# A two-block transformer: the sums of c times w_ada as chained multiply-adds on VectorE, and on ScalarE with GpSimd for eight of 28 units

## The chip, the core and the metric

The kernel runs on one core of a Trainium2 chip. A core has five engines that each work through an instruction list of their own and wait for each other by semaphores: TensorE (PE, matrix products), VectorE (DVE), ScalarE (ACT), GpSimd (POOL) and SyncE (SP), which here only issues DMAs. The metric is the time of one execution on the device, in microseconds (us).

## The reference

```python
# first block, D = 1024, 256 tokens
mod = silu(c) @ w_ada + b_ada          # (1024) x (1024 x 9216): nine vectors of 1024
sh1, sc1, gt1, sh2, sc2, gt2, sh3, sc3, gt3 = split(mod, 9)
n = rmsnorm(h, g_ffn1) * (1 + sc1) + sh1
h = h + 0.5 * gt1 * ((silu(n @ w1_gate) * (n @ w1_up)) @ w1_down)   # inner width 2816
n = rmsnorm(h, g_mix) * (1 + sc2) + sh2
h = h + gt2 * hybrid_mixer(n, w_in, w_pool, pool_scale, w_out)      # "pool" mixer below
n = rmsnorm(h, g_ffn2) * (1 + sc3) + sh3
h = h + 0.5 * gt3 * ((silu(n @ w2_gate) * (n @ w2_up)) @ w2_down)
h = rmsnorm(h, g_final)
# second block: two attention layers, with mixers called "window" and "causal", and a last norm
```

Half of the first mixer pools over windows of 2 to 16 tokens, the other half is attention with 8 heads. All is float32.

## The kernel before

All weights come through the core in units of 1 MB (128 partitions x 2048 floats): 256 columns of a weight matrix, or 256 rows of a down matrix. Unit u is loaded by SP into `raw[u % 3]` (`load_unit`), rounded to float32r by ScalarE (`whi`, `high(u)`, line 554), and VectorE makes the rest that the rounding lost (`wlo = raw - whi`, `low(u)`, line 814). TensorE then makes three products for each (`nhi,whi`, `nlo,whi`, `nhi,wlo`; lines 1133 to 1135), 48 instructions for a unit. Unit u + 3 can be loaded when `low(u)` is done, for it takes the same slot.

The stages are: eight units of w_ada at the start, a norm, the first feed-forward network (units 0 to 32: gate, up and down of eleven blocks; the blocks after the first are a loop of ten rounds, j = 0 to 9, on each engine), a norm, the pool mixer (units 33 to 44), a norm, the second feed-forward network, a norm, and the window and causal mixers.

The vector `mod` is made beside this work, in 36 units a of w_ada (each 1024 x 256, also 1 MB). Units 0 to 7 come at the start. Units 8 to 18 are needed by the end of the first feed-forward network, 19 to 31 up to the end of the pool mixer, 32 to 35 by the end of the second network. One unit takes four steps:

1. `load_ada(a)` on SP loads it into one of two slots of `ada`, and first waits until the slot's last user is summed (`macc_done`).
2. The product with silu(c), in place: on GpSimd in one instruction (line 467, `prod_done`), or, for 21, 22, 23, 25, 27, 29 and 31, on ScalarE in eight, one for each of the eight chunks of 128 rows (line 591, `aprod_done`).
3. `reduce_products(a)` on VectorE adds the eight chunks in one instruction over 128 x 2048 (line 866, into `macc`).
4. `mod_sum(a)` on TensorE sums over the partitions by two one-column products with ones (line 1163), and `mod_out` on VectorE adds b_ada.

The order within a mixer is written out by hand, once for all engines, in the list `order` of `mixer_plan`: U, K, V, Q and W are projections (each takes a unit, but W), SC the scores and the softmax of four heads, TPV transposes and the products with V, OUTA, OUTB and OUT the output projection, MACa the steps 2 and 3 of the units a and a + 1, MODa step 4 of both. Each engine does its part of each entry in this order and skips what isn't its own. After a projection ScalarE copies the result out of PSUM and then makes `high(u + 3)`, and VectorE makes `low(u + 3)`. SP's loads are in one queue, in the order of the units, with the loads of w_ada placed between them by the table `ada_after` (unit of the mixer: the units of w_ada that are loaded behind it).

Of the kernel before, what the change touches and what calls it, by code (L numbers as in the profile page):

```python
# [1537 lines left out]
```

## Time and profile before

| | |
|---|---|
| time, median of 3 runs | 897.82 us (896.24 to 899.46) |
| profiled execution: span of its instructions | 896.2 us |
| time of the profiled execution | 896.24 us, by the run that equals the span |
| TensorE busy | 767.6 us, 86% |
| VectorE busy | 620.1 us, 69% |
| ScalarE busy | 404.1 us, 45% |
| GpSimd busy | 162.6 us, 18% |
| chain that ended last, by engine | PE 68%, DVE 15%, ACT 7%, issue 6% |
| VectorE's subtractions, line 814 | 104 x 2569 ns |
| VectorE's reductions, line 866 | 32 x 3804 ns |
| moved | 152.56 MB |

A matmul's record is longer than its pitch, since matmuls overlap: within a unit one follows another every 0.12 us at the full clock. So a busy TensorE means only that it never waited. "Idle before" in a timeline names who ended the wait. Times within the span are counted from its start.

### The profile page before, as it was taken

Reading aid. Unit: us, or ns where it says so; the run is one execution under the profiler, and the core shown is the slowest. Engines: PE = TensorE matmul, PEld = TensorE weight load, DVE = VectorE, ACT = ScalarE, POOL = GpSimd, SP = SyncE. Lnnn points to the kernel's source line nnn. Section 1 sums busy time; section 2 is a strip of 40 time slices with the busy share of each in tenths; the row PEclk is TensorE's granted clock in tenths of the full one; section 3 lists DMA queues with packets and bytes.
Section 4 is the critical chain, followed back from the end, with each engine's and each line's share of the span. In section 5 each row is a group of like instructions: output and inputs, shape, how many; then the busy total and the mean of one; then the engine's idle time right before and its main releaser. Section 6 shows DMA issues by size and latency. Waiting matters only on the chain.

```text
span 896.2 us, 14391 instructions
## 1 busy us (share of the span) xinstructions
PE 767.6 (86%) x5800; PEld 720.6 (80%) x5800; DVE 620.1 (69%) x775; ACT 404.1 (45%) x645; POOL 162.6 (18%) x87
## 2 busy tenths in 40 slices
PE   4279999999959868738999999996799988999995
PEld 3279999999949866637999999994777777888884
DVE  5987877887878877677549447446567756577641
ACT  5353433343426735434444333335365553554542
POOL 3621114223245551234004000001000000000000
PEclk9579999999978978878999999998899999999998
DMA  9877777678653944065557655552133224422201
GB/s 299 269 261 240 252 248 234 222 237 270 221 173 98 325 141 142 31 222 194 189 187 234 208 189 170 184 187 93 53 119 113 94 95 141 141 95 95 95 1 47
DMA packets 132451, 152.56 MB, mean 170 GB/s; under 512 B 2616, under 2 KB 126268, under 8 KB 132284
## 3 DMA queue, kind: packets, MB, share of 16 engines
q1 hardware_dynamic: 132324, 152.01, 52.0%
q8 instruction: 26, 0.43, 0.2%
q14 instruction: 13, 0.11, 0.0%
q10 hardware_dynamic: 88, 0.02, 0.0%
HBM read 150.97 MB, written 1.05 MB: 170 GB/s over the span
## 4 chain that ended last, share of the span: by engine, by line
PE 68%; DVE 15%; ACT 7%; issue 6%; DMA 2%; POOL 1%; SPq 0%; DVEq 0%; ACTq 0%; POOLq 0%
PE sc L1133 10%; PE sc L1135 9%; PE sc L1134 9%; PE acc L1133 9%; PE acc L1134 8%; PE acc L1135 8%; DVE macc L866 6%; ACT whi L554 2%; DVE wlo L814 2%; PE stat L1144 1%; DMA ada<-in_w_ada_dram 1%; PE acc L1281 1%; DVE rstd L834 1%; PE acc L1244 1%; ACT prob L656 1%
## 5 line engine op out<-in xcount | busy, mean ns | idle before, releaser
L814 DVE TENSOR_TENSOR wlo<-raw,whi 128x2048 fp32r<-128x2048 f32 x104 | 266.9, 2569 | 110.8 <-ACT whi L554 110.8
L554 ACT ACTIVATE whi<-raw 128x2048 fp32r<-128x2048 f32 x105 | 199.9, 1905 | 80.8 <-PE sc L1135 76.5
L1133 PE MATMUL sc<-nhi,whi 128*128 128x256 f32 x704 | 202.7, 288 | 9.5 <-DVE nlo L853 6.3
L1134 PE MATMUL sc<-nlo,whi 128*128 128x256 f32 x704 | 201.2, 286 | 0.0
L1135 PE MATMUL sc<-nhi,wlo 128*128 128x256 f32 x704 | 201.2, 286 | 0.0
L1133 PEld LDWEIGHTS sc<-nhi,whi 128*128 128x128 f32 x704 | 137.4, 195 | 10.2 <-issue 6.7
L467 POOL TENSOR_TENSOR ada<-ada,cT 128x2048 f32<-128x2048 f32 x21 | 92.5, 4408 | 256.4 <-DMA ada<-in_w_ada_dram 256.4
L1134 PEld LDWEIGHTS sc<-nlo,whi 128*128 128x128 f32 x704 | 137.3, 195 | 0.0
L1135 PEld LDWEIGHTS sc<-nhi,wlo 128*128 128x128 f32 x704 | 137.1, 195 | 0.0
L1133 PE MATMUL acc<-nhi,whi 128*128 128x256 f32 x376 | 117.0, 311 | 16.6 <-DVE nlo L853 12.2
L866 DVE TENSOR_REDUCE macc<-ada 128x256 f32<-128x2048 f32 x32 | 120.8, 3804 | 5.7 <-POOL ada L467 3.4
L1134 PE MATMUL acc<-nlo,whi 128*128 128x256 f32 x376 | 110.1, 293 | 0.0
L1135 PE MATMUL acc<-nhi,wlo 128*128 128x256 f32 x376 | 109.8, 292 | 0.0
L1133 PE MATMUL acc<-hhi,whi 128*128 128x256 f32 x352 | 101.0, 287 | 4.1 <-DVE hlo L1028 4.1
L1134 PE MATMUL acc<-hlo,whi 128*128 128x256 f32 x352 | 100.2, 285 | 0.0
L1135 PE MATMUL acc<-hhi,wlo 128*128 128x256 f32 x352 | 100.0, 284 | 0.0
L1133 PEld LDWEIGHTS acc<-nhi,whi 128*128 128x128 f32 x376 | 75.8, 202 | 25.6 <-issue 18.2
L1134 PEld LDWEIGHTS acc<-nlo,whi 128*128 128x128 f32 x376 | 76.2, 203 | 1.9 <-issue 1.9
L1135 PEld LDWEIGHTS acc<-nhi,wlo 128*128 128x128 f32 x376 | 75.9, 202 | 0.0
L1133 PEld LDWEIGHTS acc<-hhi,whi 128*128 128x128 f32 x352 | 67.3, 191 | 4.5 <-DVE wlo L814 2.6
L1134 PEld LDWEIGHTS acc<-hlo,whi 128*128 128x128 f32 x352 | 67.5, 192 | 0.1
L1135 PEld LDWEIGHTS acc<-hhi,wlo 128*128 128x128 f32 x352 | 67.4, 191 | 0.0
(164 smaller groups left out, 1189.8 us busy)
## 6 DMA issues: line engine op xcount, KB each, us to landing
ada<-in_w_ada_dram SPq DMA_DIRECT2D x32, 1024.0 KB, 5.1
raw<-in_w_gate_dram SPq DMA_DIRECT2D x22, 1024.0 KB, 5.7
raw<-in_w_up_dram SPq DMA_DIRECT2D x22, 1024.0 KB, 5.4
raw<-in_w_down_dram SPq DMA_DIRECT2D x22, 1024.0 KB, 4.9
raw<-in_w_out_dram SPq DMA_DIRECT2D x12, 1024.0 KB, 5.0
raw<-in_w_in_b_dram SPq DMA_DIRECT2D x10, 1024.0 KB, 5.1
raw<-in_w_in_a_dram SPq DMA_DIRECT2D x9, 1024.0 KB, 5.3
raw<-in_w_in_dram SPq DMA_DIRECT2D x8, 1024.0 KB, 7.8
```

The lines of the kernel that those rows point to most:

```text
L467: nc.gpsimd.tensor_tensor(to, to, c_mul, ALU.mult).then_inc(prod_done, 1)
L554: nc.scalar.activation(whi[:, u % NS], raw[:, u % NS], ACT.Copy).then_inc(hi_done, 1)
L656: ins = nc.scalar.activation(prob[:, s, lo:up], prob[:, s, lo:up], ACT.Exp, bias=nm[:, s, b:b + 1], accum_out=den[:, s, b:b + 1])
L814: nc.vector.tensor_tensor(wlo[:, u % NS], raw[:, u % NS], whi[:, u % NS].bitcast(F32), ALU.subtract).then_inc(lo_done, 1)
L834: link(nc.vector.reciprocal(rstd[:, :], std[:, :]))
L866: nc.vector.tensor_reduce(macc[:, slot], src.rearrange("p c n -> p n c"), AX_X, ALU.add).then_inc(macc_done, 1)
L1133: mm(to, stat_hi, mov_hi, start=first, stop=False, skip_group_check=True)
L1134: mm(to, stat_hi, mov_lo, start=False, stop=False, skip_group_check=True)
L1135: return mm(to, stat_lo, mov_hi, start=False, stop=last, skip_group_check=True)
L1144: mm(ss_ps, ones[:, :], src, start=first, stop=last).then_inc(ss_done, 1)
L1244: mm(rot_ps[:, :], rotation, src[:, :, :].rearrange("p b n -> p (b n)"), start=True, stop=True).then_inc(rot_done, 1)
L1281: mm(to[part, 0:S], vv[:, 0, col:col + HD], probT[:, h % 2, 0:S], start=True, stop=False, skip_group_check=True)
```

## The change

Three things are changed.

Most units of w_ada from 8 on (`BY_DVE`: 8 to 19, 24, 26, 28, 30 and 32 to 35) are now made on VectorE alone by `multiply_add`: one multiplication by c of the first chunk, and seven `scalar_tensor_tensor` (chunk times c plus the sum so far), each of 128 x 256 and each waiting for the one before (`part_done`). No product on GpSimd or ScalarE is made for them. The other eight (`BY_POOL`: 20 to 23, 25, 27, 29, 31) have their product on ScalarE, as eight instructions, and the sum on GpSimd, as three additions of 1024, 512 and 256 elements in a partition (`add_parts`), with semaphores of their own. Units 20 to 23 move from the mixer into the first feed-forward loop: ScalarE makes their products behind its rounds 0, 3, 5 and 7, and SP's loop is cut behind its rounds 2, 4 and 6 for the loads of 21, 22 and 23. The mixer's list and the table of loads are new.

```diff
-            order = ["U0", "MAC20", "U1", "K0", "MOD20", "MAC22", "K1", "V0", "MOD22", "MAC24", "Q0", "V1",
-                     "SC0", "W0", "W1", "MOD24", "MAC26", "Q1", "TPV0", "SC1", "OUTA", "MOD26", "TPV1", "MAC28",
-                     "OUTB", "OUT1", "MOD28", "MAC30", "OUT2", "MOD30", "OUT3"]
+            order = ["U0", "MAC24", "U1", "K0", "MOD24", "K1", "MAC26", "V0", "Q0", "MOD26", "V1", "SC0", "W0", "W1",
+                     "MAC28", "Q1", "TPV0", "SC1", "OUTA", "MOD28", "TPV1", "MAC30", "OUTB", "OUT1", "MOD30", "OUT2",
+                     "OUT3"]
-ADA_SLOT = {a: 1 if 9 <= a < 20 else a % 2 for a in range(MOD_START, MOD_UNITS)}
+BY_POOL = (20, 21, 22, 23, 25, 27, 29, 31)
+BY_DVE = tuple(a for a in range(MOD_START, MOD_UNITS) if a not in BY_POOL)
+ADA_SLOT = {a: 0 if a in BY_POOL or a in (8, 32, 34) else 1 for a in range(MOD_START, MOD_UNITS)}
...
# SP, load_ada: the wait for the slot's last user
+                if n in BY_POOL:
+                    sp.wait_ge(pmacc_done, BY_POOL.index(n) + 1)
+                elif n is not None:
+                    sp.wait_ge(macc_done, MOD_START + BY_DVE.index(n) + 1 + (reps if reps is not None else 0))
# SP, first feed-forward network
+                    load_ada(20)
                     sp.dma_start(consts[:, P:C_END], shape_consts[:, P:C_END]).then_inc(tables_in, 16)
-                for start, end in ((1, FB - 1),) if first else ((0, 4), (4, FB - 1)):
+                for start, end in ((1, 3), (3, 5), (5, 7), (7, FB - 1)) if first else ((0, 4), (4, FB - 1)):
...
+                    if first and end < FB - 1:
+                        load_ada(21 + (end - 3) // 2)
...
-                    ada_after = {3 * FB: (19,), 3 * FB + 1: (20,), 3 * FB + 2: (21,), 3 * FB + 5: (22, 23), 3 * FB + 7: (24, 25),
-                                 3 * FB + 9: (26, 27), 3 * FB + 10: (28, 29), 3 * FB + 11: (30, 31)}
+                    ada_after = {3 * FB: (19,), 3 * FB + 1: (24,), 3 * FB + 2: (25,), 3 * FB + 4: (26, 27),
+                                 3 * FB + 6: (28, 29), 3 * FB + 9: (30, 31)}
# GpSimd
-            product(8)
-            product(9)
-            with pool.Fori(0, FB - 1) as j:
-                product(10, reps=j)
+            for a in (20, 21, 22, 23):
+                add_parts(a)
...
+            def add_parts(a):
+                part, n = ada[:, ADA_SLOT[a]], BY_POOL.index(a)
+                pool.wait_ge(aprod_done, MOD_START // 2 + n + 1)
+                link(nc.gpsimd.tensor_tensor(part[:, 0:4], part[:, 0:4], part[:, 4:8], ALU.add))
+                link(nc.gpsimd.tensor_tensor(part[:, 0:2], part[:, 0:2], part[:, 2:4], ALU.add))
+                if n >= 2:
+                    pool.wait_ge(pmod_cols, n - 1)
+                nc.gpsimd.tensor_tensor(macc[:, 2 + n % 2], part[:, 0], part[:, 1], ALU.add).then_inc(pmacc_done, 1)
# ScalarE, first feed-forward loop
+                for start, end in ((0, 1), (1, 4), (4, 6), (6, 8), (8, FB - 1)) if f == 0 else ((0, FB - 1),):
...
+                    if end < FB - 1:
+                        product({1: 20, 4: 21, 6: 22, 8: 23}[end])
# VectorE
+            def multiply_add(a, reps=None):
+                n, add = BY_DVE.index(a), reps if reps is not None else 0
+                part, to = ada[:, ADA_SLOT[a]], macc[:, macc_slot(a)]
+                dve.wait_ge(ada_in[ADA_SLOT[a]], ada_landings(a) + 16 * add)
+                dve.wait_ge(mod_cols, MOD_START + n - 1 + (1 if reps is not None else 0) + add)
+                for ch in range(DC):
+                    if ch == 0:
+                        ins = nc.vector.tensor_scalar(to, part[:, ch], cT[:, ch:ch + 1], None, ALU.mult)
+                    else:
+                        dve.wait_ge(part_done, 7 * n + ch + 7 * add)
+                        ins = nc.vector.scalar_tensor_tensor(out=to, in0=part[:, ch], scalar=cT[:, ch:ch + 1], in1=to,
+                                                             op0=ALU.mult, op1=ALU.add)
+                    if ch < DC - 1:
+                        ins.then_inc(part_done, 1)
+                ins.then_inc(macc_done, 1)
# TensorE, first feed-forward loop, cut behind rounds 2, 5, 7 and 9
+                    if f == 0:
+                        n = {3: 0, 6: 1, 8: 2, FB - 1: 3}[end]
+                        mod_sum(20 + n, mod3_ps[:, 2 * n:2 * n + 2])
```

Besides, `fgain` (the last norm's gain) now lies in a slot of `ada` and is loaded ahead of the causal mixer, and `mod_out(20, 4)` writes the four moved units behind the first network.

SP's queue in the first feed-forward loop. Before, from the loop's start to its end (lines 370 are weight units, 378 a unit of w_ada):

```order
L370 ISA [waits lo_done]
L370 DMA raw<-in_w_gate_dram 128x8x256
L369 REGISTER_ALU
L370 DMA raw<-in_w_up_dram 128x8x256 [waits lo_done]
L369 REGISTER_ALU
L370 ISA [waits lo_done]
L370 DMA raw<-in_w_down_dram 128x2x1024
L377 REGISTER_ALU
L378 ISA [waits macc_done]
L378 DMA ada<-in_w_ada_dram 128x8x256
L414 REGISTER_ALU
L414 COMPARE_AND_BRANCH
```

Now, from the middle of round 4 (the second of the four loops) to the start of round 5 (386 are weight units, 397 units of w_ada):

```order
L386 DMA raw<-in_w_down_dram 128x2x1024
L396 REGISTER_ALU
L397 ISA [waits macc_done]
L397 DMA ada<-in_w_ada_dram 128x8x256
L434 REGISTER_ALU
L434 COMPARE_AND_BRANCH
L397 DMA ada<-in_w_ada_dram 128x8x256 [waits pmacc_done]
L434 UNCONDITIONAL_BRANCH
L434 ISA
L386 ISA [waits lo_done]
L386 DMA raw<-in_w_gate_dram 128x8x256
```

A load that waits for GpSimd's sum of the unit before (`pmacc_done`) now stands between the weight units of round 4 and those of round 5. The same stands behind rounds 2 and 6.

SP's queue in the pool mixer, from the load of unit 35 (K0) on. Before:

```order
L370 DMA raw<-in_w_in_dram 128x8x256 [waits lo_done]
L378 DMA ada<-in_w_ada_dram 128x8x256 [waits macc_done]
L370 DMA raw<-in_w_in_dram 128x8x256 [waits lo_done] x3
L378 DMA ada<-in_w_ada_dram 128x8x256 [waits macc_done] x2
L370 DMA raw<-in_w_in_dram 128x8x256 [waits lo_done] x2
L378 DMA ada<-in_w_ada_dram 128x8x256 [waits macc_done] x2
L370 DMA raw<-in_w_out_dram 128x8x256 [waits lo_done] x2
L378 DMA ada<-in_w_ada_dram 128x8x256 [waits macc_done] x2
```

Now:

```order
L386 DMA raw<-in_w_in_dram 128x8x256 [waits lo_done]
L397 DMA ada<-in_w_ada_dram 128x8x256 [waits pmacc_done]
L386 DMA raw<-in_w_in_dram 128x8x256 [waits lo_done] x2
L397 DMA ada<-in_w_ada_dram 128x8x256 [waits macc_done]
L397 DMA ada<-in_w_ada_dram 128x8x256 [waits pmacc_done]
L386 DMA raw<-in_w_in_dram 128x8x256 [waits lo_done] x2
L397 DMA ada<-in_w_ada_dram 128x8x256 [waits macc_done]
L397 DMA ada<-in_w_ada_dram 128x8x256 [waits pmacc_done]
L386 DMA raw<-in_w_in_dram 128x8x256 [waits lo_done]
```

Unit 38 (Q0) stood ahead of the first pair of w_ada and now stands behind one (26, 27); unit 40 (Q1) stood ahead of the second pair and now stands behind it (28, 29).

VectorE in the same place, from `low(36)` behind U0 to the softmax. Before:

```order
L814 TENSOR_TENSOR wlo<-raw,whi 128x2048 [waits hi_done,tables_in]
L866 TENSOR_REDUCE macc<-ada 128x256 [waits mod_cols,prod_done]
L866 TENSOR_REDUCE macc<-ada 128x256 [waits mod_cols,aprod_done]
L814 TENSOR_TENSOR wlo<-raw,whi 128x2048 [waits hi_done] x2
L875 TENSOR_TENSOR mod<-sc,biasT 128x4 [waits mod_cols]
L866 TENSOR_REDUCE macc<-ada 128x256 [waits mod_cols,aprod_done] x2
L814 TENSOR_TENSOR wlo<-raw,whi 128x2048 [waits hi_done] x2
```

Now:

```order
L838 TENSOR_TENSOR wlo<-raw,whi 128x2048 [waits hi_done,tables_in]
L897 TENSOR_SCALAR macc<-ada,cT 128x256 [waits mod_cols,ada_in1]
L900 SCALAR_TENSOR_TENSOR macc<-ada,cT,macc 128x256 [waits part_done] x7
L838 TENSOR_TENSOR wlo<-raw,whi 128x2048 [waits hi_done] x2
L923 TENSOR_TENSOR mod<-sc,biasT 128x4 [waits mod_cols,pmod_cols]
L838 TENSOR_TENSOR wlo<-raw,whi 128x2048 [waits hi_done]
L897 TENSOR_SCALAR macc<-ada,cT 128x256 [waits mod_cols,ada_in1]
L900 SCALAR_TENSOR_TENSOR macc<-ada,cT,macc 128x256 [waits part_done] x7
L838 TENSOR_TENSOR wlo<-raw,whi 128x2048 [waits hi_done] x2
L923 TENSOR_TENSOR mod<-sc,biasT 128x4 [waits mod_cols,pmod_cols]
```

Two reductions have become a chain of eight instructions, and `low(39)` now stands ahead of the second of them.

## Rows read from the trace of the kernel before

**Rows 1.** Busy time by stretch; columns: stretch, length, PE, PEld, DVE, ACT, POOL, PEclk, DMA share, GB/s.

```profile
59.00:268.00 209.00, 197.92 (x1598) 196.25 (x1598) 167.53 (x92) 76.31 (x65) 56.69 (x19) 0.97 0.72 238
268.00:418.00 150.00, 109.33 (x731) 99.58 (x731) 115.24 (x133) 75.53 (x148) 61.90 (x43) 0.83 0.53 172
```

**Rows 2.** Waits of PE from 262 to 420; columns: us in total, times, longest.

```profile
PE sc L1163 <- DVE macc L866: 15.5, 5, 11.5
PE sc L1163 <- DVE mx L926: 11.7, 2, 6.8
```

**Rows 3.** Timeline, first network, rounds 3 and 4; columns: start, us, instruction, idle before.

```profile
129.36 0.37 SPq L378 DMA_DIRECT2D ada<-in_w_ada_dram  x1
131.60 0.37 SPq L370 DMA_DIRECT2D raw<-in_w_gate_dram  x1
...
138.69 1.90 ACT L554 ACTIVATE whi<-raw 128x2048 fp32r<-128x2048 f32 x1
144.85 1.90 ACT L554 ACTIVATE whi<-raw 128x2048 fp32r<-128x2048 f32 x1
...
142.90 3.87 DVE L866 TENSOR_REDUCE macc<-ada 128x256 f32<-128x2048 f32 x1
146.79 2.29 DVE L814 TENSOR_TENSOR wlo<-raw,whi 128x2048 fp32r<-128x2048 f32 x1
...
155.53 0.50 PE L1163 MATMUL stat<-ones,macc 128*128 128x1 f32 x4
155.90 0.36 PE L1133 MATMUL sc<-nhi,whi 128*128 128x256 f32 x1
```

**Rows 4.** ScalarE's eight products of one unit, and the landing of w_ada's loads.

```profile
279.47 3.30 ACT L591 ACTIVATE ada<-ada,cT 128x256 f32<-128x256 f32 x8
...
DMA to landing us min/median/max: 4.9/5.1/10.1
```

**Rows 5.** Busy time by stretch, behind TensorE's waits (ended 246.9 and 311.9).

```profile
247.00:250.00 3.00, 3.00 (x15) 3.00 (x16) 3.00 (x1) 1.05 (x2) 3.00 (x1) 0.50 0.59 185
307.00:313.00 6.00, 3.19 (x26) 2.87 (x24) 2.58 (x2) 5.12 (x10) 3.45 (x1) 0.88 1.09 347
313.00:316.00 3.00, 3.00 (x15) 2.50 (x12) 3.00 (x2) 0.47 (x1) 0.00 (x0) 0.50 0.19 45
316.00:322.00 6.00, 6.00 (x45) 5.87 (x45) 5.79 (x12) 0.33 (x1) 1.26 (x2) 0.81 0.96 322
```

**Rows 6.** Timeline, GpSimd against VectorE, by a norm behind the second network.

```profile
621.26 0.85 POOL L476 TENSOR_TENSOR std<-sq 128x256 f32<-128x256 f32 x1 [7.36 <-ACT sq L565]
...
621.45 0.95 DVE L842 SCALAR_TENSOR_TENSOR hT<-hT,gainT,rstd 128x256 f32<-128x256 f32 x1
...
L842 DVE SCALAR_TENSOR_TENSOR hT<-hT,gainT,rstd x8: 473/480/947, 619.9 to 624.0; 128x256 f32<-128x256 f32 x8
```

**Rows 7.** Timeline, ends of the start and of the first network.

```profile
53.16 3.60 POOL L467 TENSOR_TENSOR ada<-ada,cT 128x2048 f32<-128x2048 f32 x1 [6.98 <-DMA ada<-in_w_ada_dram]
54.64 6.47 DVE L814 TENSOR_TENSOR wlo<-raw,whi 128x2048 fp32r<-128x2048 f32 x2 [1.39 <-ACT whi L554]
58.96 0.58 PE L1133 MATMUL sc<-nhi,whi 128*128 128x256 f32 x1 [3.19 <-DVE wlo L814]
...
246.63 5.69 DVE L814 TENSOR_TENSOR wlo<-raw,whi 128x2048 fp32r<-128x2048 f32 x1
```

**Rows 8.** Timeline, pool mixer.

```profile
281.88 7.68 DVE L866 TENSOR_REDUCE macc<-ada 128x256 f32<-128x2048 f32 x2
283.34 0.61 POOL L510 TENSOR_TENSOR pw<-pw 128x256 f32<-128x256 f32 x1
...
358.70 4.47 DVE L946 TENSOR_SCALAR prob<-prob,rden 128x128 f32<-128x128 f32 x2
399.50 0.99 PE L1163 MATMUL sc<-ones,macc 128*128 128x1 f32 x4 [11.54 <-DVE macc L866]
411.62 0.88 DVE L828 SCALAR_TENSOR_TENSOR hT<-acc,mod,hT 128x256 f32<-128x256 f32 x2 [1.31 <-PE acc L1135]
```

More of the change, by code:

```diff
@@ L157, in by_act, with macc_slot @@
 def by_act(a):
-    return (a < MOD_START or 20 <= a < 32) and a % 2 == 1 or a == 22
+    return a % 2 == 1
 def products(a, act):
     return sum(by_act(n) == act for n in range(a + 1))
+def macc_slot(a):
+    if a < MOD_START:
+        return a % 2
+    if a in BY_POOL:
+        return 2 + BY_POOL.index(a) % 2
+    return 1 if 9 <= a < 20 else BY_DVE.index(a) % 2
 def slot_before(a):
-    return max([n for n in range(MOD_START, a) if ADA_SLOT[n] == ADA_SLOT[a]], default=-1) + 1
+    return max([n for n in range(MOD_START, a) if ADA_SLOT[n] == ADA_SLOT[a]], default=None)
 FFN_UNIT = (0, 3 * FB + 12)
@@ L192, in build @@
         ada = sb("ada", [P, 2, DC, UC])
-        macc = sb("macc", [P, 2, UC])
+        macc = sb("macc", [P, 4, UC])
         hT = sb("hT", [P, DC, S])
@@ L519, in pooling @@
                 pool.wait_ge(pooled, g + 1)
-            product(20)
             add_squares(1)
@@ L536, in _ @@
                         bias(h)
-                elif st["kind"] == "MAC" and st["i"] > 20 and not by_act(st["i"]):
-                    product(st["i"])
+                elif st["kind"] == "MAC":
+                    add_parts(st["i"] + 1)
             add_squares(2)
-            for a in range(32, MOD_UNITS):
-                product(a)
             for k in range(3, 6):
@@ L706, in mixer @@
                     elif st["kind"] == "MAC":
-                        if by_act(st["i"]):
-                            product(st["i"])
                         product(st["i"] + 1)
@@ L855, in normalise, with reduce_products @@
                                                        op1=ALU.subtract).then_inc(nlo_done, 1)
-            def reduce_products(a, reps=None):
-                add = reps if reps is not None else 0
-                dve.wait_ge(aprod_done if by_act(a) else prod_done, products(a, by_act(a)) + add)
-                slot = a % 2 if a < MOD_START else ADA_SLOT[a]
-                last = max([n for n in range(a) if (n % 2 if n < MOD_START else ADA_SLOT[n]) == slot], default=-1)
-                if last >= 0:
-                    dve.wait_ge(mod_cols, last + 1 + add)
-                src = start_slots[a % 5] if a < MOD_START else ada[:, slot]
-                nc.vector.tensor_reduce(macc[:, slot], src.rearrange("p c n -> p n c"), AX_X,
-                                        ALU.add).then_inc(macc_done, 1)
+            def reduce_products(a):
+                dve.wait_ge(aprod_done if by_act(a) else prod_done, products(a, by_act(a)))
+                if a >= 2:
+                    dve.wait_ge(mod_cols, a - 1)
+                nc.vector.tensor_reduce(macc[:, a % 2], start_slots[a % 5].rearrange("p c n -> p n c"), AX_X,
+                                        ALU.add).then_inc(macc_done, 1)
@@ L869, in mod_out @@
             def mod_out(a, count=2, reps=None):
                 n = 2 * count
-                dve.wait_ge(mod_cols, a + count + (reps if reps is not None else 0))
-                ps = mod0_ps if a == 0 else (mod2_ps if 19 <= a < 32 and reps is None or a == 34 else mod1_ps)[:, 0:n]
+                if a == 20 or a in (24, 26, 28, 30):
+                    dve.wait_ge(pmod_cols, BY_POOL.index(a + count - 1) + 1)
+                if a >= MOD_START and a != 20:
+                    dve.wait_ge(mod_cols, MOD_START + BY_DVE.index(a if a < 32 else a + 1) + 1 +
+                                (reps if reps is not None else 0))
+                elif a == 0:
+                    dve.wait_ge(mod_cols, MOD_START)
@@ L874, in mod_out @@
+                if a == 0:
+                    ps = mod0_ps
+                elif a == 20:
+                    ps = mod3_ps
+                else:
+                    ps = (mod2_ps if 19 <= a < 32 and reps is None or a == 34 else mod1_ps)[:, 0:n]
                 at = 2 * a if reps is None else reps * 2 + 2 * a
@@ L1068, in ffn @@
                     mod_out(19, 1)
-                    dve.wait_ge(mod_done, 20)
+                    mod_out(20, 4)
+                    dve.wait_ge(mod_done, 24)
                     link(coefficient(1))
@@ L1158, in mod_sum @@
             def mod_sum(a, to, reps=None):
-                pe.wait_ge(macc_done, a + 1 + (reps if reps is not None else 0))
-                slot = a % 2 if a < MOD_START else ADA_SLOT[a]
+                if a in BY_POOL:
+                    pe.wait_ge(pmacc_done, BY_POOL.index(a) + 1)
+                else:
+                    n = a if a < MOD_START else MOD_START + BY_DVE.index(a)
+                    pe.wait_ge(macc_done, n + 1 + (reps if reps is not None else 0))
+                slot = macc_slot(a)
                 for n in range(2):
@@ L1440, in ffn @@
                     mod_sum(8, mod1_ps[:, 0:2])
-                for start, end in ((0, FB - 1),) if f == 0 else ((0, 3), (3, FB - 1)):
+                for start, end in ((0, 3), (3, 6), (6, 8), (8, FB - 1)) if f == 0 else ((0, 3), (3, FB - 1)):
                     with pe.Fori(start, end) as j:
```

66 lines of the change are left out of this document (34 added, 32 removed).

## The prediction, written before the changed kernel ran

> **What bounds the kernel now.** I read the stretches first, then TensorE's waits, then the timelines of the engines on which those waits end, and last the two instruction queues that the diff cuts. In the first network TensorE is busy for 197.9 of 209 us at a granted clock of 0.97 [rows 1]: it sets the pace, and whatever VectorE, ScalarE or GpSimd save inside its loop is worth nothing, while whatever makes a weight unit late there costs in full. The pool mixer is the opposite: TensorE works 109.3 of 150 us, VectorE 115.2 [rows 1], and TensorE's two largest waits are for `macc`, 15.5 us, and for the softmax's maxima, 11.7 us [rows 2]. There a change in the sums of w_ada can gain.
>
> **The chain of eight against the reduction.** An in-place reduction has a pitch of 7.68 / 2 = 3.84 us [rows 8]. A `scalar_tensor_tensor` of 128 x 256 takes 0.48 us [rows 6], and the next must wait for it; with some 0.04 us between two that is 0.52, times seven 3.64, and the first multiplication at most 0.48: about 4.1 us. So on VectorE one unit costs what it cost before, +0.3 us, and the gain lies in the count: the mixer now has four units on VectorE instead of twelve (24, 26, 28, 30), and no product in front of them. Bounds: 3.2 us if the eight overlapped like independent ones, 5 us if the wait costs twice 0.04 and the loop's register instructions are not hidden.
>
> But these instructions read two SBUF operands. With a GpSimd addition beside it, such an instruction took 0.95 instead of 0.48 us [rows 6]: 0.47 us more for an addition of 256 elements (0.61 us in this form [rows 8]). The reductions at 281.88 took 3.84 us each while GpSimd worked in short steps beside them [rows 8], the same as elsewhere. Now GpSimd's sum is three additions: 0.61 us for 256 elements [rows 8] and 3.60 for 2048 [rows 7] give 1.67 ns an element, so 1.9, 1.0 and 0.6 us, 3.8 with gaps. Where both run they take turns, one chained step for one GpSimd instruction. The Trainium skill ("SBUF — State Buffer", Who interferes with whom) says this as a rule: a DVE instruction with two SBUF inputs and a GpSimd instruction that reads SBUF block each other fully, a reduction never contends. By that rule the change trades a form that never waits for one that does; the row at 621.45 agrees.
>
> **First network, start: -2.1 us.** The product of unit 8 (3.60 us from 53.16) held up `low(1)`, two of which took 6.47 us instead of 4.4, and TensorE waited for it until 58.96 [rows 7]. Without that product TensorE starts 2.0 to 2.1 us earlier. SP's queue now waits for unit 8's sum before `load_ada(20)`; the units behind it land some 2 us later, which the 7 us between a unit's rounding and its use cover.
>
> **Its loop, TensorE's own part: +1.1 us.** `mod_sum` takes 0.37 us (155.53 to 155.90 [rows 3]); three of the four new ones stand inside, the fourth falls into the wait behind the loop.
>
> **Its loop, SP's queue: +15.0 us.** This term decides. SP runs ahead of ScalarE: behind its round 4 (w_ada at 129.36) it issues unit 17 at 131.60 [rows 3], as soon as `low(14)` has freed the slot. In the changed kernel `load_ada(22)` stands between, and waits for GpSimd's sum of unit 21. Its product is behind ScalarE's round 3, whose last `high(16)` runs from 138.69 to 140.6 [rows 3]; eight products take 3.30 us [rows 4], so 143.9; the sum takes 3.8 us, with VectorE's own chain beside it (the reduction stood at 142.90 [rows 3]) 4.8: 148.7. Unit 22 lands 5.1 us later [rows 4], unit 17 behind it: 1.05 MB at 347 GB/s [rows 5] is 3.0 us, so 156.9. Then 1.9 us for `high` and 2.3 for `low` with their gaps: 161.1. TensorE wants it at 155.90 [rows 3]: it waits 5.2 us. Today `high(17)` runs at 144.85. After such a wait the clock is at half: granted 0.50 for at least 3.0 us behind a wait of 2.5, and 0.50 then 0.81 over 9 us behind one of 3.0 [rows 5], which costs 1.6 to 3.2 us; I take 2.3. Behind round 6 it is the same again (`load_ada(23)` waits for unit 22's sum, behind ScalarE's round 5). Behind round 2 it is not: unit 20's product follows round 0, and its sum is done before SP arrives. So 2 x (5.2 + 2.3) = 15.0. Bounds: with no turns taken and a late loss of 1.6, 2 x (4.2 + 1.6) = 11.6; with 3.3 us for a megabyte and 3.2 for the clock, 2 x (6 + 3.2) = 18.4.
>
> **End of the loop: -2.6 us.** The last `low` took 5.69 us beside a GpSimd product [rows 7], 3.4 more than alone; without it the chain for unit 19 (+0.3) ends earlier, and with it the residual, by about 3.5 us of which 0.9 are already in the two small terms above.
>
> **Pool mixer: +9.0 us.** All times here are counted as in the trace of before, as if the mixer began where it does there. `low(36)` ends at 281.9, where the reductions began [rows 8]. The chain for unit 24 now meets GpSimd's pooling (0.61 us a step) and its sum of unit 25: eight steps, eight turns, end at 291.2 instead of 286.0; sum 25 at 291.7. Only then does SP load 26, 27, and behind them units 38 and 39, which land at 302.2 and 305.1. VectorE stands in `low(38)`, then `low(39)` (309.3), then the chain for 26 beside sum 27: 316.4. Behind that SP loads 28, 29, 40, 41; unit 41 lands at 330.3, `low(41)` ends at 334.5, and only after it `mod_out(26)`, for which the scores wait: 334.7, against 311.9 before [rows 5]: +22.8. Then it gains: GpSimd's product no longer holds the softmax (-2.7). Unit 43 is the third such victim (behind 30 and 31, which wait for 28 and 29): ScalarE has `high(43)` before the second softmax, now +26.8. That softmax gains 3.0: its scaling took 4.47 us beside a product [rows 8]. +23.7 when unit 30's chain begins; it ends at 404.1. TensorE's waits of 11.5 us [rows 8] and 2.4 are gone, and three output steps of residual, `high` and `low`, 5.5 us each, lead to the last residual at 420.6, against 411.62 [rows 8]: +9.0. The same walk with no turns taken gives scores at +15.8 and the last residual at 408.4: -3.2. With 3.3 us a megabyte it is +12.
>
> **The rest: 0.** In the second network the same number of units is on VectorE, TensorE never waits there today, and units 32 to 35 have no GpSimd work beside them. The two attention layers keep their instructions; the gain's load is 0.5 MB where DMA is mostly idle.
>
> Sum: -2.1 + 1.1 + 15.0 - 2.6 + 9.0 = +20.4 on the span of 896.2 of an execution that itself took 896.2, so 916.6; the median of the runs is 1.6 us above that one: 918.
>
> **Rivals.** *The loads come late, but taking turns costs nothing.* For it: the row at 621.45 is one pair of small instructions. Against it: it fits. 11.6 - 3.2 - 3.6 = +4.8: 903. *The loop is covered, the mixer is not.* This needs unit 17 to have 5 us more slack than rows 3 give; against it the order of the queue, which is fixed. -3.6 + 9.0 = +5.4: 903. *Faster: TensorE is not held in the loop and the mixer keeps its gain.* One mechanism, the slack of the weight units: if loads issued 17 us late still arrive before TensorE needs them (a pair of units deep in `raw` and `whi`), only the savings are left: -3.6 - 3.2 = -6.8, so 891. It decides when unit 17 lands before 151.7; that needs sum 21 at 143.6, before its product is even done at 143.9. For it speaks only that the mixer's waits for `macc` (15.5 us) and GpSimd's 92 us of products vanish. *The chain costs 5 us instead of 4.1*: in the loop VectorE has over 3 us of idle time a round, in the mixer +1 for each of four: 921.
>
> **Chances.** Forecast (both late loads and turns taken) 0.60, either of the two alone 0.22, faster 0.15, otherwise slower 0.03. Three runs of this kernel tell about 0.3% (2.7 us). The range must reach over the two at 903 and leaves out the faster one: 902 to 926. Faster by over 0.3%: 0.15; within: 0.03; slower: 0.82.
>
> **What the profile would show.** In the first network: SP's units 17 and 23 issued about 17 us after the rhythm, TensorE waiting some 5 us for `wlo` before two of ten rounds, and a lower clock behind both. GpSimd's additions and VectorE's chained steps stretched to 0.9 us and more wherever they meet. In the mixer: `high(38)`, `high(40)` and `high(43)` ended by a DMA, scores of the first softmax some 20 us late against the mixer's start, no wait of 11 us before the last output step. I am wrong if TensorE runs through the loop, or if the chained steps stay at 0.5 us beside GpSimd.

## The result, and the profile after

The changed kernel takes 914.4 us (median of 4 runs, 913.6 to 915.8) against 898.6 us (896.2 to 899.6) for the kernel before in the same session: ratio 1.0186, 95% interval 1.0168 to 1.0205. It is slower by 15.8 us; the forecast was 918 us, range 902 to 926.

In the changed kernel's profile the lines have new numbers: L838 is `low`, L577 `high`, L897 and L900 VectorE's chain, L491, L492 and L495 GpSimd's three additions, L614 ScalarE's products, L386 and L397 the loads of weight units and of w_ada, L1216 `mod_sum`, L923 `mod_out`, L852 the residual, L1313 the scores. Among the costliest groups (busy time, mean ns of one | idle before) the chain shows its price at once: 140 steps, 666 ns each on the mean, though a step alone takes some 480.

```profile
L900 DVE SCALAR_TENSOR_TENSOR macc<-ada,cT,macc 128x256 f32<-128x256 f32 x140 | 93.2, 666 | 5.0
```

Busy time by stretch (columns of [rows 1]): the first stretch of [rows 1], the mixer from norm to norm, and the stretches behind TensorE's two long waits of the loop:

```profile
59.00:268.00 209.00, 193.57 (x1588) 192.86 (x1587) 146.68 (x167) 87.10 (x89) 19.37 (x12) 0.97 0.70 233
275.93:431.94 156.01, 105.33 (x714) 95.77 (x714) 85.59 (x148) 65.20 (x123) 51.46 (x49) 0.81 0.46 147
...
159.60:163.00 3.40, 3.40 (x20) 3.40 (x19) 3.05 (x3) 2.76 (x3) 0.00 (x0) 0.58 1.10 351
202.70:206.00 3.30, 3.23 (x15) 3.24 (x16) 3.20 (x3) 3.11 (x3) 0.00 (x0) 0.50 1.06 343
```

GpSimd and VectorE have much less to do than before (GpSimd 19.4 instead of 56.7 us in the first stretch, VectorE 85.6 us in the mixer, where it had 115.2 from 268 to 418 [rows 1]), yet TensorE is busy for less of the first stretch: the time went into waits. Behind the two long ones its clock was granted at 0.58 and 0.50, so for most of these stretches at the lower of its two levels: matmuls start every 0.21 us instead of 0.12, which costs 1.5 us behind the first wait (until 162.4) and 1.9 us behind the second (until 206.8). TensorE's waits from 60 to 270, then from 262 to 460 (us in total, times, longest), where [rows 2] had `macc` and `mx`:

```profile
PE sc L1182 <- DVE wlo L838: 11.8, 2, 6.3
...
PE sc L1313 <- DVE mod L923: 17.6, 1, 17.6
PE sc L1313 <- DVE mx L974: 9.3, 1, 9.3
PE acc L1182 <- ACT kraw L648: 6.7, 1, 6.7
```

The first wait of the loop, followed backwards through the timeline of the changed kernel, at the place of [rows 3]:

```profile
126.50 20.30 SPq L397 DMA_DIRECT2D ada<-in_w_ada_dram  x2
147.13 0.37 SPq L386 DMA_DIRECT2D raw<-in_w_gate_dram  x1
...
138.02 3.29 ACT L614 ACTIVATE ada<-ada,cT 128x256 f32<-128x256 f32 x8
154.69 1.91 ACT L577 ACTIVATE whi<-raw 128x2048 fp32r<-128x2048 f32 x1 [12.21 <-DMA raw<-in_w_gate_dram]
...
141.39 2.69 POOL L491 TENSOR_TENSOR ada<-ada 128x1024 f32<-128x1024 f32 x1 [48.50 <-ACT ada L614]
144.16 1.35 POOL L492 TENSOR_TENSOR ada<-ada 128x512 f32<-128x512 f32 x1
145.59 0.80 POOL L495 TENSOR_TENSOR macc<-ada 128x256 f32<-128x256 f32 x1
...
122.70 3.61 DVE L900 SCALAR_TENSOR_TENSOR macc<-ada,cT,macc 128x256 f32<-128x256 f32 x7
140.81 6.91 DVE L900 SCALAR_TENSOR_TENSOR macc<-ada,cT,macc 128x256 f32<-128x256 f32 x7
141.85 2.51 DVE L900 SCALAR_TENSOR_TENSOR macc<-ada,cT,macc 128x256 f32<-128x256 f32 x1
156.63 2.29 DVE L838 TENSOR_TENSOR wlo<-raw,whi 128x2048 fp32r<-128x2048 f32 x1 [8.91 <-ACT whi L577]
...
159.06 0.58 PE L1182 MATMUL sc<-nhi,whi 128*128 128x256 f32 x1 [5.49 <-DVE wlo L838]
```

SP's two w_ada loads span 20.3 us, because the second stands until GpSimd's sum of unit 21 ends at 146.4; only then is unit 17 issued (147.13; before, 131.60 [rows 3]). ScalarE gets it 12.2 us after it ran out of work, TensorE 5.5 us after it wanted it. The chain without a GpSimd sum beside it takes 3.61 us for seven steps (122.70), beside one 6.91 (140.81). The third step of that chain, 141.85, alone took 2.51 us: it ends only when GpSimd's long addition (141.39, 2.69 us) has ended.

In the mixer the same thing stands in front of the first scores:

```profile
300.50 4.22 SPq L397 DMA_DIRECT2D ada<-in_w_ada_dram  x2
304.76 1.86 SPq L386 DMA_DIRECT2D raw<-in_w_in_dram  x2
326.88 0.99 SPq L397 DMA_DIRECT2D ada<-in_w_ada_dram  x2
327.92 1.42 SPq L386 DMA_DIRECT2D raw<-in_w_in_dram  x1
...
312.51 1.92 ACT L577 ACTIVATE whi<-raw 128x2048 fp32r<-128x2048 f32 x1 [12.04 <-DMA raw<-in_w_in_dram]
338.11 1.91 ACT L577 ACTIVATE whi<-raw 128x2048 fp32r<-128x2048 f32 x1 [17.08 <-DMA raw<-in_w_in_dram]
...
301.67 2.65 POOL L495 TENSOR_TENSOR macc<-ada 128x256 f32<-128x256 f32 x1
...
293.94 6.53 DVE L900 SCALAR_TENSOR_TENSOR macc<-ada,cT,macc 128x256 f32<-128x256 f32 x7
300.39 3.35 DVE L838 TENSOR_TENSOR wlo<-raw,whi 128x2048 fp32r<-128x2048 f32 x1
406.07 6.63 DVE L900 SCALAR_TENSOR_TENSOR macc<-ada,cT,macc 128x256 f32<-128x256 f32 x7
428.80 0.87 DVE L852 SCALAR_TENSOR_TENSOR hT<-acc,mod,hT 128x256 f32<-128x256 f32 x2
...
345.58 0.81 PE L1313 MATMUL sc<-kd,qT 64*128 64x128 f32 x4 [17.61 <-DVE mod L923]
```

Units 38 and 40 reach ScalarE 12 and 17 us after it ran out of work, each loaded (304.76 and 327.92) behind a w_ada pair that waited for a chain and a sum. GpSimd's last addition, of 256 elements (0.61 us alone [rows 8]), took 2.65 us against a `low` of 2048 elements, and that `low` 3.35 instead of 2.29.

To compare kernels I cut each profiled run where ScalarE takes the root of a norm (the `std` rows; before at 264.90, 413.83 and 617.56, changed at 275.93, 431.94 and 635.67). Each number in this table is a difference of two such rows, the last one of the span and the third row.

| kernel | first network | pool mixer | second network | rest | median, us |
|---|---|---|---|---|---|
| before | 264.9 | 148.9 | 203.7 | 278.6 | 898.6 |
| changed | 275.9 | 156.0 | 203.7 | 276.9 | 914.4 |
| e1, products early | 260.0 | 156.1 | 203.7 | 276.9 | 900.4 |
| e2, mixer's loads later | 277.1 | 132.0 | 203.9 | 276.8 | 890.7 |
| e3, both | 261.6 | 132.2 | 203.9 | 276.7 | 875.3 |
| e4, before with the chain alone | 261.9 | 149.0 | 203.8 | 276.9 | 895.2 |
| e5, e3, TensorE takes four units | 260.9 | 135.1 | 204.0 | 279.4 | 880.8 |
| e6, e3, one addition of three | 259.8 | 121.2 | 203.9 | 276.9 | 864.9 |
| e7, e3, chain before K1 | 260.5 | 131.5 | 204.0 | 279.0 | 875.5 |
| e8, e3, MOD24 later | 259.7 | 128.4 | 203.8 | 276.9 | 874.0 |
| e9, changed, one addition of three | 263.4 | 143.8 | 204.8 | 278.2 | 892.0 |
| e10, e8, reductions in the mixer | 260.1 | 129.0 | 205.2 | 277.9 | 872.5 |

The stretches behind the mixer move by up to 3 us between runs of kernels whose code there is the same, so they carry no cause, and a difference below that between two medians is not read as one either. The first network moves too: e1, e3, e5, e7, e8 and e10 have the same code there and took 259.7 to 261.6 us, a spread that arises for the most part ahead of the loop (VectorE's first chain starts at 58.91 in e1 and at 60.20 in e3). The mixer agrees within 0.2 us where its code is the same (changed and e1, e2 and e3). The change costs +11.0 us in the first network and +7.1 in the mixer.

### The profile page after: what moved, and what is told of

It reads as the page before. It is cut to its first block, busy times and chain, and to the rows that moved or that the text cites. A ratio compares the mean times of both kernels' runs of the same rounds, so it can differ in the third digit from the quotient of the medians.

```text
span 912.6 us, 14572 instructions
## 1 busy us (share of the span) xinstructions
PE 764.7 (84%) x5800; PEld 717.6 (79%) x5800; DVE 569.0 (62%) x906; ACT 407.6 (45%) x653; POOL 104.3 (11%) x90
## 4 chain that ended last, share of the span: by engine, by line
PE 43%; ACT 4%; DVE 4%; issue 1%; POOL 0%; DVEq 0%; ACTq 0%; POOLq 0%
PE acc L1182 6%; PE acc L1183 6%; PE acc L1184 6%; PE sc L1182 5%; PE sc L1184 5%; PE sc L1183 5%; PE stat L1193 1%; PE acc L1334 1%; PE acc L1297 1%; PE acc L1376 1%; PE acc L1377 1%; PE acc L1378 1%; ACT whi L577 1%; DVE rstd L858 1%; ACT prob L679 1%
## 5 line engine op out<-in xcount | busy, mean ns | idle before, releaser
L838 DVE TENSOR_TENSOR wlo<-raw,whi 128x2048 fp32r<-128x2048 f32 x104 | 239.2, 2301 | 171.9 <-ACT whi L577 171.8
L577 ACT ACTIVATE whi<-raw 128x2048 fp32r<-128x2048 f32 x105 | 200.0, 1905 | 137.0 <-PE sc L1184 62.9
L1182 PE MATMUL sc<-nhi,whi 128*128 128x256 f32 x704 | 203.7, 289 | 19.1 <-DVE wlo L838 12.8
L900 DVE SCALAR_TENSOR_TENSOR macc<-ada,cT,macc 128x256 f32<-128x256 f32 x140 | 93.2, 666 | 5.0
L504 POOL TENSOR_TENSOR std<-sq 128x256 f32<-128x256 f32 x5 | 3.8, 759 | 365.9 <-ACT sq L588 365.9
```

Of the source, the lines that this page charges most:

```text
L577: nc.scalar.activation(whi[:, u % NS], raw[:, u % NS], ACT.Copy).then_inc(hi_done, 1)
L838: nc.vector.tensor_tensor(wlo[:, u % NS], raw[:, u % NS], whi[:, u % NS].bitcast(F32), ALU.subtract).then_inc(lo_done, 1)
L900: ins = nc.vector.scalar_tensor_tensor(out=to, in0=part[:, ch], scalar=cT[:, ch:ch + 1], in1=to, op0=ALU.mult, op1=ALU.add)
L1182: mm(to, stat_hi, mov_hi, start=first, stop=False, skip_group_check=True)
```

## The experiments

**e1: only ScalarE's products move.**

```
-  for start, end in ((0, 1), (1, 4), (4, 6), (6, 8), (8, FB - 1)) if f == 0 ...
+  for start, end in ((0, 1), (1, 3), (3, 5), (5, 7), (7, FB - 1)) if f == 0 ...
-      product({1: 20, 4: 21, 6: 22, 8: 23}[end])
+      product({1: 20, 3: 21, 5: 22, 7: 23}[end])
```

> The changed kernel, only ScalarE's products of units 20 to 23 stand behind its rounds 0, 2, 4 and 6 of the first network instead of 0, 3, 5 and 7, so that the sums of 21 and 22 are done when SP's queue reaches the w_ada loads that wait for them. Theory A (two w_ada loads hold the weight units in SP's queue): both waits of TensorE for wlo in the loop (11.8 us with the one at 159.06 and the one at 202.76) go, and with them the low clock behind each (about 2 x 1.5 us); the first network ends about 14 us earlier, the mixer is as long as it was, time near 900 us. Rival B (what the loop lost is VectorE's chain taking turns with GpSimd's sums and ScalarE's 3.3 us products in the way): the same four products and sums still stand in the loop, so no more than 3 us come back, 911 us.

Measured: 900.4 us, ratio to before 1.002 (1.0002 to 1.0038). TensorE's waits from 60 to 262, all that there are:

```profile
PE sc L1216 <- DVE macc L900: 2.8, 1, 2.8
PE stat L1193 <- POOL std L504: 2.6, 1, 2.6
PE acc L1182 <- DVE hlo L1075: 0.8, 1, 0.8
```

Both waits for `wlo` are gone, though all four products and sums still stand in the loop and four of its chains still take 6.9 us. The first network ends 16.0 us earlier than in the changed kernel: 11.8 us of waits, 3.3 us of lower clock behind them (1.5 and 1.9), and 0.7 us by which this run entered the loop earlier (first chain at 58.91, changed 59.60); 0.2 us is left over. By the medians the gain is 14.1 us. Theory A holds: with the product one round earlier, the sums and their chains cost TensorE no wait in the loop, though they are as long as before.

**e2: only the mixer's w_ada loads move, and e3: both.**

```
-  3 * FB + 4: (26, 27), 3 * FB + 6: (28, 29), 3 * FB + 9: (30, 31)}
+  3 * FB + 6: (26, 27), 3 * FB + 9: (28, 29), 3 * FB + 11: (30, 31)}
```

> The changed kernel, only the mixer's w_ada pairs stand further back in SP's queue: (26, 27) behind unit 39 instead of 37, (28, 29) behind 42 instead of 39, (30, 31) behind 44 instead of 42. Theory A: TensorE's wait of 17.6 us before the first scores goes nearly whole, since units 38 to 41 no longer wait for the sums of 24 to 27; the waits behind it (6.7 and 9.3 us) shrink too; 18 us less, 896 us, with the loop's stalls as they were. Rival B (the mixer is held by the chained steps that take turns with GpSimd, not by the loads): each chain stays beside a sum of GpSimd and takes 6.5 to 7 us as now, the first scores move by under 5 us, 909 us.

> Both of the above. The places are 100 us apart, so under theory A the gains add: 14 + 18 = 32 us, 882 us, which would be 16 us faster than the kernel before. Rival: the mixer's gain is covered in part once the loop is quick (other clock); 888 us.

Measured: e2 890.7 us, ratio 0.990 (0.987 to 0.993); e3 875.3 us, ratio 0.974 (0.970 to 0.977). TensorE's waits in e2's mixer that answer to the changed kernel's 17.6 and 9.3, and the one for GpSimd's sum (3.2 there); the 6.7 us for `kraw` are as they were:

```profile
PE sc L1313 <- DVE mod L923: 3.5, 1, 3.5
...
PE sc L1216 <- POOL macc L495: 3.3, 1, 3.3
PE sc L1313 <- DVE mx L974: 2.9, 1, 2.9
```

The mixer is 24.0 us shorter than the changed kernel's, and 17 shorter than the one before, which is what the change gives when its loads do not stand in the way. I had said 18: the maxima's wait (9.3 to 2.9, unit 43 no longer late) gave more than I allowed. In e3 the two gains add up (16 + 24 = 40 in theory, 39.1 measured). Rival B failed in e2: the chains are still 6.5 and 6.9 us long there.

**e4: the kernel before, with the chain alone.** Units 8 to 19 and 32 to 35 by VectorE's chain, GpSimd's products of them gone (shortened):

```
+  CHAIN = tuple(range(8, 20)) + tuple(range(32, 36))
   def reduce_products(a, reps=None):
+      if a in CHAIN: ... tensor_scalar, then seven scalar_tensor_tensor as in multiply_add
-  product(8); product(9); with pool.Fori(0, FB - 1) as j: product(10, reps=j)    # GpSimd
```

> The kernel before, with one part of the change alone: units 8 to 19 and 32 to 35 are summed by VectorE's chain of eight instead of GpSimd's product and a reduction; the mixer, the order of the loads and the units in each loop are as before. By my terms the start gains 2.1 us and the end of the first network's loop 2.6 us, the chain's own 0.3 us a unit is hidden: 894 us. Rival (a chain of waits is dear, 5 us or more a unit, and the loop feels it): 898 us or above.

Measured: 895.2 us, ratio 0.996 (0.994 to 0.998). The chain is worth a small gain by itself; the rival is out. The first network gains 3.0 us, less than the 4.7 of my two terms. The loop's end shows a reason (VectorE, then GpSimd):

```profile
243.12 5.55 DVE L812 TENSOR_TENSOR wlo<-raw,whi 128x2048 fp32r<-128x2048 f32 x1 [1.11 <-ACT whi L552]
...
242.91 3.60 POOL L471 TENSOR_TENSOR ada<-ada,cT 128x2048 f32<-128x2048 f32 x1 [200.60 <-DMA ada<-in_w_ada_dram]
```

GpSimd's product of unit 20, the mixer's first, now starts here and takes the place of the loop's last one: `low` waits again, 5.55 us instead of 2.29. In the changed kernel unit 20 is summed inside the loop, so this cannot happen there: its last `low` (260.34) takes 2.29 us. With nothing held in the loop (e1 and the five others) the first network gains 3.3 to 5.2 us against before; my small terms said 2.1 - 1.1 + 2.6 = 3.6. The 1.7 us by which e4 falls short lie within the spread between runs, so its rows show the mechanism and not what it costs.

**e9: the changed kernel, with one GpSimd addition of three.**

```
-  link(nc.gpsimd.tensor_tensor(part[:, 0:4], part[:, 0:4], part[:, 4:8], ALU.add))
-  link(nc.gpsimd.tensor_tensor(part[:, 0:2], part[:, 0:2], part[:, 2:4], ALU.add))
```

> The changed kernel as it is, with GpSimd's first two additions of each of the eight sums left out (those sums hold two of eight parts); the order of the loads is untouched. My prediction's terms: turns cost 12.2 us of the mixer (+9.0 with them, -3.2 without) and 2 x 1.0 us of the loop's waits; here the sum of a unit is 0.8 instead of 4.8 to 6.9 us, which also brings each blocked load 3 us forward. So the loop loses 2 x 4 us less, the mixer 12 us less: 896 us. Rival (turns were over-sized by me: the mixer measured +6.2 instead of +9.0 and each pair's load waits for VectorE's chain anyway): 4 us in the loop, 5 in the mixer, 905 us.

Measured: 892.0 us, ratio to before 0.994 (0.993 to 0.996), so 22.5 us less than the changed kernel. This kernel leaves out two of three additions, so its sums hold two of eight parts. TensorE's waits, loop and mixer:

```profile
PE sc L1180 <- DVE wlo L836: 2.3, 2, 1.3
...
PE sc L1311 <- DVE mod L921: 17.7, 1, 17.7
PE sc L1311 <- DVE mx L972: 9.0, 1, 9.0
```

The mixer is 12.3 us shorter; I had put the turns at 12.2, but e9 takes away more than turns: each sum's own 4 us go as well. The loop gives back 12.5 instead of 8: 9.5 us of waits, and most of the 3.3 us of lower clock, which did not follow waits of 1.0 and 1.3 us. The long waits for `mod` and `mx` stay, since the pairs still stand in front of the units. The rival's 905 is out. What the two long additions cost (their length and the turns together) comes on top of the late loads: 12.3 us of the mixer here, 11.0 with the loads moved (e6). How much of it is turns alone, no run shows.

**e6: the same on e3.**

> Built on the kernel with both moves. Of GpSimd's three additions for each of the eight units only the last (256 elements) is done; the first two, of 1024 and 512 elements, are left out, so those sums hold two of eight parts. Theory A (one chained step waits for one GpSimd addition, the long ones above all): the four chains of the mixer fall from 6.5 to 6.9 us to about 4.2; each pair is ready 2.5 us earlier; of the four places the waits of TensorE before the first scores (3.5 us) and for the maxima (2.9 us) give some back: 871 us. Rival B (turns cost nothing, chains are long for another reason): chains stay at 6.5 us, time within 1 us of 875.

Measured: 864.9 us, ratio 0.963 (0.960 to 0.966). The mixer's four chains took 4.88, 4.33, 4.09 and 4.05 us instead of 6.53, 6.92, 6.50 and 6.63, as theory A said, but the mixer lost 11.0 us, not 4. I had looked at the chains alone. In e3 GpSimd's sum also runs beside `low` (2.65 us for its last addition), and TensorE waits 3.3 us for the sum itself at MOD24; in e6 that wait is gone, one of 3.3 us for ScalarE's `sq` at the norm behind the mixer is 1.3, and the mixer's mean granted clock is 0.89 instead of 0.85. The wait before the first scores, where I had looked for a gain, is 4.2 instead of 3.5 us.

**e5: TensorE takes units 25, 27, 29 and 31 itself.**

```
+  if a in BY_PE:
+      for n in range(2):
+          for ch in range(DC):
+              ins = mm(to[:, n:n + 1], ada[:, 0, ch, n * P:(n + 1) * P], cT[:, ch:ch + 1],
+                       start=(ch == 0), stop=(ch == DC - 1))
```

> Built on the kernel with both moves. Units 25, 27, 29 and 31 of the mixer are taken by TensorE straight from w_ada (sixteen matmuls with one column of c each, added up in PSUM) instead of ScalarE's eight products, GpSimd's three additions and two matmuls with ones. Theory A (VectorE's chain takes turns with GpSimd's sum: 6.5 to 6.9 us for seven steps beside it, 3.61 alone): with no sum beside them all four chains of the mixer show 3.6 us; ScalarE loses 13 us of products; TensorE gets 4 x 14 matmuls more, at about 0.2 us each some 11 us, mostly while it would wait anyway: 872 us against 875. Rival B (the long chains come from the DMA traffic or ScalarE's work, not from GpSimd): chains stay at 6.5 us, and TensorE's 11 us are added, 884 us.

ScalarE's products and GpSimd's sums of these four units are gone too.

Measured: 880.8 us, ratio 0.980 (0.978 to 0.983), 5.5 us slower than e3; of this the mixer shows 2.9, the rest lies behind it, where the code is the same. Two rows of VectorE from the timeline of e5's mixer, and one of its groups by line (busy time, mean ns of one | idle before):

```profile
302.87 3.62 DVE L899 SCALAR_TENSOR_TENSOR macc<-ada,cT,macc 128x256 f32<-128x256 f32 x7
339.83 3.61 DVE L899 SCALAR_TENSOR_TENSOR macc<-ada,cT,macc 128x256 f32<-128x256 f32 x7
```

```profile
L1212 PE MATMUL sc<-cT,ada 128*128 128x1 f32 x128 | 17.3, 269 | 0.0
```

The 64 matmuls are 128 records, two each. Three of the four chains fell to 3.6 us with the loads unchanged (the first, beside GpSimd's pooling, to 4.76), so the DMA traffic had not stretched them; nor had ScalarE, since in e6 its products stand and the chains fall too. But TensorE paid 17.3 us instead of my 11, in a place where it was not only waiting. Both theories failed on the sum; the mechanism of A held, its price of a matmul did not.

**e7 and e8: other places for MAC26 and MOD24.**

```
   e3:  "K0", "MOD24", "K1", "MAC26", "V0"
   e7:  "K0", "MAC26", "K1", "MOD24", "V0"
   e8:  "K0", "K1", "MOD24", "MAC26", "V0"
```

> Built on the kernel with both moves. In the mixer's order, MAC26 stands before K1 and MOD24 behind it (K0, MAC26, K1, MOD24, V0 instead of K0, MOD24, K1, MAC26, V0). TensorE waited 3.25 us at MOD24 for GpSimd's sum of unit 25 (290.20) and ran 4 us at half clock behind it, and VectorE was idle from 292.4 to 301.4 while the chain of 26 came later at 303.98. My theory (the turns reach TensorE through this wait for the sum and through the first scores' wait of 3.5 us for the sum of 27): both waits go and about 2 us of low clock with them, 9 us, 866 us. Rival (the mixer is set by ScalarE's queue and the softmax): under 2 us, 874.

> Built on the kernel with both moves. Only MOD24 moves one job back (K0, K1, MOD24, MAC26, V0), so TensorE asks for the sums of 24 and 25 one job of 6 us later. My theory: the waits of 0.68 and 3.25 us and 2 us of low clock behind them go, the chain of 26 starts 5 us earlier since K1 does: 5 us, 870 us. Rival (what is won before the first scores is lost in their wait for the sum of 27, now longer): under 2 us, 874.

Measured: e7 875.5 us, ratio 0.976 (0.972 to 0.980), which is no gain on e3; e8 874.0 us, 0.975 (0.972 to 0.979). e8's mixer is 3.7 us shorter in its profiled run, but the medians cannot tell it from e3. Its rival is borne out: the wait of `mod` before the first scores fell from 3.5 to 0.4 us, and the one for GpSimd's sums grew from 3.3 to 7.5, now for the sum of 27.

```profile
PE sc L1216 <- POOL macc L495: 7.5, 1, 7.5
```

What I had missed is in GpSimd's and VectorE's rows of e7:

```profile
302.63 4.28 POOL L491 TENSOR_TENSOR ada<-ada 128x1024 f32<-128x1024 f32 x1
306.98 3.19 POOL L492 TENSOR_TENSOR ada<-ada 128x512 f32<-128x512 f32 x1
...
301.94 2.75 DVE L838 TENSOR_TENSOR wlo<-raw,whi 128x2048 fp32r<-128x2048 f32 x1
306.35 2.71 DVE L838 TENSOR_TENSOR wlo<-raw,whi 128x2048 fp32r<-128x2048 f32 x1 [1.65 <-ACT whi L577]
```

With the chain out of the way the sum of 27 meets two `low`s, and its first two additions take 7.5 us instead of 3.9; TensorE waits 6.8 us for it in place of the 3.3 for the sum of 25. The wait was moved, not removed.

**e10: e8 with VectorE's reductions in place of GpSimd's sums in the mixer.**

```
   elif kind == "MAC":
       multiply_add(st["i"])
+      reduce_parts(st["i"] + 1)      # tensor_reduce over the eight products, VectorE
-      add_parts(st["i"] + 1)         # GpSimd
```

> Built on the kernel of e8 (both moves and MOD24 one job later). In the mixer VectorE sums ScalarE's products of units 25, 27, 29 and 31 by one reduction each (3.84 us in the kernel before) behind its own chain, and GpSimd's three additions are gone. Theory A (a chained step and a weight unit's subtraction take turns with GpSimd's additions, a reduction does not): the chains fall from 5.0 to 6.5 us to about 4 beside the pooling steps, the sum of 25 is ready 8 us after the first chain begins instead of 11, the waits for it (7.5 us in all in e8) halve; VectorE does 15 us more, of which about 10 come back from shorter chains and subtractions: 869 us against 874. Rival B (VectorE's added 15 us are on the path, since it is the mixer's busiest engine but TensorE): 882 us.

Measured: 872.5 us (871.5 to 874.0), ratio 0.971 (0.969 to 0.973): the fastest of those that compute everything, 26 us below before and 42 below the changed kernel, though not to be told from e8. VectorE's four reductions take 15.2 us, but its busy time in the mixer rises only from 86.4 (e8) to 90.7, since its chains and subtractions are shorter, and nothing is lost by it. Rival B is out, and so is most of my gain: the 7.5 us for GpSimd's sum went, but TensorE now waits 4.0 us for `mod` (0.4 in e8) and 7.5 for `kraw` (6.7). The rows of VectorE and of GpSimd's pooling show why a reduction is a good neighbour:

```profile
282.83 3.93 DVE L909 TENSOR_REDUCE macc<-ada 128x256 f32<-128x2048 f32 x1
286.66 4.93 DVE L836 TENSOR_TENSOR wlo<-raw,whi 128x2048 fp32r<-128x2048 f32 x2
...
282.70 1.37 POOL L536 TENSOR_TENSOR pw<-pw 128x256 f32<-128x256 f32 x2
286.90 5.98 POOL L536 TENSOR_TENSOR pw<-pw 128x256 f32<-128x256 f32 x3
```

Beside the reduction two of GpSimd's steps take 1.37 us; beside the two `low`s three of them take 5.98.

## Why the prediction was right

- *The loop's queue, +15.0.* The term that decided. I had GpSimd's sum of unit 21 at 148.7, TensorE waiting 5.2 us twice and 2.3 us of low clock each. It was 146.4, waits of 5.5 and 6.3 us, and 1.5 and 1.9 us of clock: 15.1 us in all. That the sum comes so close is partly luck: the waits were 1.4 us longer than I had them, the clock 1.3 us cheaper. The sum took 5.0 us (4.8 predicted) and came 2.3 us sooner than I had it because the whole loop runs some 2 us earlier, which I had booked at the start; TensorE wants the unit as much earlier, at 153.6 (159.06 less its wait), so the wait is what I had.
- *Start -2.1, loop's own part +1.1, loop's end -2.6.* Together -3.6; measured -3.3 to -5.2 (the six kernels without a wait for `wlo` in the loop against before). e4's rows show that the end's gain depends on unit 20 having left it.
- *Pool mixer, +9.0.* Measured +7.1 between the norms. The first scores came at 345.58, 11.0 of which are the late start: +22.6 against 22.8 predicted. Two errors on the way there cancel: the first chain ended at 300.5, 1.8 us sooner than I had it (291.2 + 11.0), and sum 25 at 304.3, 1.6 us later (291.7 + 11.0). Behind the scores my walk was 2 us too long: the last chain ended at 412.7, not at 404.1 + 11.0. By the last residual (428.80), to which the forecast counted, the mixer is +6.2. Which step behind the first softmax was too long, I did not find.
- *Turns.* I had put them at 12.2 us of the mixer. No run separates them: e9's 12.3 and e6's 11.0 hold the length of the additions too. That they exist the rows show: the step at 141.85 took 2.51 us, and the whole stretch of a chain beside a sum (3.3 us) in the loop goes to the three steps that meet an addition (141.85 and the two behind it), not to all seven. Chain alone 3.61 us for seven steps and 0.34 for the first, against 4.1 predicted; beside a sum 6.5 to 6.9. The Trainium skill ("SBUF — State Buffer", Who interferes with whom) has VectorE instructions with two SBUF inputs shut out GpSimd's that read SBUF and a reduction never. e10's rows, 5.98 for three steps beside `low` and 1.37 for two beside the reduction, agree.
- *The rest, 0.* The second network 203.7 in both. What lies behind it was 1.7 us shorter, which the table shows to be the spread of single runs. The forecast span of 916.6 measured 912.6: 0.4 us less in the first network, 1.9 in the mixer, 1.7 here.
- *The rivals.* "Turns cost nothing" asks for chains of 3.6 us beside a sum, and they took 6.9. "The loop is covered" asks for no wait for `wlo`. "Faster, by the slack of the weight units" asked for unit 17 before 151.7; ScalarE could take it at 154.69. "The chain costs 5 us": 3.95.

What I did not see is how cheap the cure was. I called the queue's order a cost of the change, yet moving three product calls and three pairs of loads brought back 39 us (e3), and with the queues so ordered the changed kernel is 24 us faster than the one before.

## What to carry to other kernels

When a load waits for a sum, write down what stands behind it in the same queue and when each is needed: a load in the wrong place holds every one behind it, and moving it back past those whose buffers are free sooner cost nothing here. Ask for the producer's place too: three products one round earlier gave 14 to 16 us (e1). Do not put two-operand work on VectorE and GpSimd at the same time where either is waited for; count such a pair as one engine, and try a reduction on VectorE before giving GpSimd the sum (e10).

## What the runs showed of the hardware that I had not expected

- The exclusion reaches further than the chain: GpSimd's 256-element addition took 2.65 us against a `low` that had the lead (2.29 us alone), and the 1024- and 512-element additions 4.28 and 3.19 us (e7) where they take 2.4 to 2.7 and 1.3 to 1.4 beside a chain. In these rows long instructions make worse neighbours than short ones.
- The chain's first multiplication reads one tensor only (the chunk; c is its scalar), and is held as well: in the changed kernel's mixer it took 0.83 us and ended only after a GpSimd step that ran until 293.74; alone it takes 0.34 or 0.35.

```profile
291.04 2.70 POOL L543 TENSOR_TENSOR tmp<-pw,tmp 128x256 f32<-128x256 f32 x1
293.07 0.83 DVE L897 TENSOR_SCALAR macc<-ada,cT 128x256 f32<-128x256 f32 x1
```

- A chained step waits for a semaphore of its own engine at a pitch of 0.516 us (3.61 / 7) against 0.48 for the instruction, wherever no GpSimd work is beside it: eight dependent steps (3.95 us) cost about as much as a reduction's 3.84 us, and do the product besides.
- A matmul with one moving column and a 128 x 128 f32 operand to load took 0.27 us, 17.3 us for 64 of them (e5).
- Behind waits of 1.0 and 1.3 us before a unit (e9) the clock was granted in full; behind those of 5.5 and 6.3 us matmuls started every 0.21 us for 3.4 and 4.0 us, 16 and 18 of them, which at 0.12 us each is a loss of 1.5 and 1.9 us. The row is e9's, by stretch, behind the longer of its two:

```profile
155.00:163.00 8.00, 8.00 (x68) 8.00 (x69) 7.24 (x10) 4.36 (x5) 0.00 (x0) 1.00 1.09 350
```
